# Summing the squares of three RMS norms with one strided VectorE reduction in place of seven GpSimd additions each

## The chip, the cores and the metric

The kernel runs on one core of one Trainium2 chip. The metric is the time of one execution on the device in microseconds (us); lower is better. The core has five engines that run side by side and wait for one another on semaphores: TensorE (PE in the profile, its weight loads are PEld), VectorE (DVE), ScalarE (ACT), GpSimd (POOL) and SyncE (SP), which issues most of the DMAs.

## The reference, cut to what matters

Three transformer blocks run one after the other on 512 tokens of width 1024, all in fp32: a differential attention block with an MLP, a latent attention block with an MLP, and a block of mixers with a gated MLP (SwiGLU) and a gated side input. Between them stand RMS norms over the 1024 features of a token:

```python
def rms_norm(x, g, eps=EPS):
    xf = x.astype(jnp.float32)
    y = xf * lax.rsqrt(jnp.mean(xf * xf, axis=-1, keepdims=True) + eps)
    return (y * g.astype(jnp.float32)).astype(x.dtype)

hn = rms_norm(h, attn_norm_g[0]); qkv = hn @ w_qkv_a[0]               # norm 0, first product
f = swiglu(rmsnorm(x, g_ffn_pre), w_gate_up, w_down)                  # norm 9, gate/up
gate = jax.nn.sigmoid(rmsnorm(x, g_ple) @ w_ple_gate)                 # norm 11, last gate
x = x + gate * (p @ w_ple_proj)
```

The change concerns how the sum of the squares of x over its features is made for these three norms (of twelve).

## The kernel before, in words

**Layout.** Activations lie transposed: the feature is the partition, and a tensor of 1024 features by 512 tokens is `h[128, 8, 512]`, eight tiles `h[:, k, :]` (KD = 8). An RMS norm is not applied ahead of its product. The product is made of the unscaled x, and the factor rstd, one number for each token, is multiplied into its result. So rstd is made while TensorE works, in these steps: eight tiles of squares (ACT); their sum over k, `ssq[128, 512]`; `stat` (L549): matmuls with a column of ones, which add up over the 128 partitions; `mean_square` (L1408, DVE); `rstd` (L2032, POOL, a power of -0.5); `broadcast` (L558): matmuls that spread rstd over all partitions; `take_rstd` (L1412, DVE), a copy into `rstd_f`.

**fp32 by three products.** Every operand is split into a high part of type fp32r and a low remainder. ACT makes the high part (`hi` L949 for weights, `x_hi` L961 for activations), DVE the low one (`lo` L1396, a `tensor_tensor` over 128x2048 at L1399; `x_lo` L1402, a `scalar_tensor_tensor` over 128x512 at L1405, eight for one norm). A product is three matmuls (L480 to L482). The first chunk of a stage goes in another order, as its x is fresh: for each k the two products with the high part of x (L519, L520), two output tiles at a time, and only then sixteen products with the low parts (L530), each pair behind its own `x_lo`.

**Weights.** They come in 149 chunks of 128x2048 fp32, each good for 48 matmuls, into two slots in turn. SP loads (L386), ACT writes `whi`, DVE writes `wlo`, TensorE waits for `wlo_done`. Each engine works through an order written out by hand; an engine that waits holds up all that is behind on it.

**Around the change.** In norms 0, 9 and 11 the order on TensorE is: first chunk c with its L530 tail; chunk c + 1, with `late_rstd` (L568) as a hook in it: `stat` ahead of its k = 3 (so behind 18 matmuls), and `broadcast` ahead of k = 4 for norm 0 and of k = 6 for norms 9 and 11. On DVE it is: eight `x_lo`; `lo(c + 1)`; for norm 0 some small operations (L1433 to L1442, one of them behind an exponential on ACT), `mean_square`, `lo(c + 2)`, `take_rstd`, two tables and a `rope`; for norms 9 and 11 `lo(c + 2)`, `mean_square`, `take_rstd` and the scaling of the product's tiles. On ACT the squares are L968 (norm 0) and L1329 (norms 9 and 11). On POOL `add_squares` (L2036) adds the tiles of squares one after another, seven additions at L2042, and ends with `rstd`; for norms 9 and 11 it stands behind four residual additions (L2171). The other norms are summed on POOL as well (norm 8 and 10 by `add_squares` too).

```python
for k in range(1, KD):
    pool.wait_ge(sq_done, SQ[n] + k + 1)
    if k >= 2:
        pool.wait_ge(ssq_done, SSQ[n] + k - 1)
    pool.tensor_tensor(ssq[:, :], squares[:, 0, :] if k == 1 else ssq[:, :], squares[:, k, :],
                       ALU.add).then_inc(ssq_done, 1)
rstd(n)
```

Of the kernel before, what the change touches and what calls it, by code (L numbers as in the profile page):

```python
# [16 lines left out]
ALU = mybir.AluOpType  # L17
ACT = mybir.ActivationFunctionType
AX = mybir.AxisListType
# [5 lines left out]
KD = D // P  # L25
# [47 lines left out]


SQUARED = (8, 8, 8, 2, 3, 8, 16, 0, 8, 8, 8, 8)
ADDED = (7, 7, 7, 1, 2, 7, 14, 0, 7, 7, 7, 7)
N_NORMS = len(SQUARED)
SQ = [sum(SQUARED[:n]) for n in range(N_NORMS + 1)]
SSQ = [sum(ADDED[:n]) for n in range(N_NORMS + 1)]
STATS = [n if n < 7 else n - 1 for n in range(N_NORMS)]  # L80
# [41 lines left out]
def build(nc, wst, xT, gains, cos, sin, ident_in, mask_in, lam, pT_in, tab_in, buckets_in, pool_w_in, pool_fix_in, outT):  # L122
    ctx = ExitStack()
    with ctx:
        def sem(name):
            return ctx.enter_context(nc.semaphore(name))
# [4 lines left out]
        def at(name, shape, dt, offset):  # L131
            return nc.alloc_sbuf_tensor_at(name, shape, dt, offset=offset)

        def sb(name, shape, dt=F32):
            n = (2 if dt == BF16 else 4) * int(np.prod(shape[1:]))
            t = at(name, shape, dt, base[0])
            base[0] += (n + 31) // 32 * 32
            assert base[0] <= top, (name, base[0], top)
            return t
# [14 lines left out]
        sq_tmp, ssq = sb("sq_tmp", [P, S]), sb("ssq", [P, S])  # L154
# [41 lines left out]
        squares0 = at("squares0", [P, KD, S], F32, xb_at + 16 * K)  # L196
# [15 lines left out]
        squares = at("squares", [P, KD, S], F32, G + 48 * K)  # L212
# [11 lines left out]
        squares2 = at("squares2", [P, KD, S], F32, G)  # L224
# [64 lines left out]
        sq_done = sem("sq_done")  # L289
        ssq_done = sem("ssq_done")  # L290
# [71 lines left out]
        def g(name, k):  # L362
            c0 = GAINS[name][0] + k
            return gain[:, c0:c0 + 1]
# [112 lines left out]
        def _(pe):  # L477
# [357 lines left out]
            def scores2(jb, tiles):  # L835

                q, k, _, hd = JOBS[jb]
                rows = slice(64 * (hd % 2), 64 * (hd % 2) + 64)
                for i in tiles:
                    tt = T_JOB[jb] + i  # L840
                    bank_ready(tt)
                    if jb % 2 == 0 and i == 0:
                        for tile in Q_TILES[jb // 2]:
                            pe.wait_ge(bank_free[tile % 4], tile // 4 + 1)
                    out, chosen = ps[tt % 4][:, 0:P * (i + 1)], jb >= 4 and i >= 1
                    mm = pe.matmul(out, q[rows, hd // 2, P * i:P * i + P], k[rows, hd // 2, 0:P * (i + 1)],  # L846
                                   start=True, stop=not chosen)
                    if chosen:
                        pe.wait_ge(sel_done, i)
                        mm = pe.matmul(out, ident_b[:, :], sel[:, IDX_OFF[i]:IDX_OFF[i] + P * (i + 1)],  # L850
                                       start=False, stop=True)
                    mm.then_inc(tile_done, 1)

            def weighted2(jb):
                _, _, v, hd = JOBS[jb]
                n = 2 * HEADS + jb
                if jb in (0, 4):
                    for tile in V_TILES[jb // 4]:
                        pe.wait_ge(bank_free[tile % 4], tile // 4 + 1)
                pe.wait_ge(on_done, HEADS + jb)  # L860
                for j, i in enumerate(TR_ORDER):
                    pe.wait_ge(ptc_done, 4 * n + j + 1)
                    for kt in range(i + 1):
                        mm = pe.matmul(O_PS[:, i * 64:(i + 1) * 64],  # L864
                                       pT2[:, OFF[i] + kt * P:OFF[i] + (kt + 1) * P],
                                       v[:, kt, 64 * hd:64 * hd + 64], start=(kt == 0), stop=(kt == i))
                mm.then_inc(o_done, 1)
# [527 lines left out]
        def _(dve):  # L1395
            def lo(c, slot):  # L1396

                dve.wait_ge(whi_done, c + 1)
                dve.tensor_tensor(wlo[slot][:, :], raw[slot][:, :], whi[slot][:, :].bitcast(F32),  # L1399
                                  ALU.subtract).then_inc(wlo_done, 1)  # L1400

            def x_lo(dst, src, scale, dst_hi, n):  # L1402

                dve.wait_ge(xh_done, n + 1)
                dve.scalar_tensor_tensor(out=dst, in0=src, scalar=scale, in1=dst_hi.bitcast(F32),  # L1405
                                         op0=ALU.mult, op1=ALU.subtract).then_inc(xl_done, 1)

            def mean_square(n, dim):  # L1408
                dve.wait_ge(stat_done, STATS[n] + 1)
                dve.tensor_scalar(ms_t[:, 4 * n:4 * n + 4], STAT[:, 0:QT], 1.0 / dim, EPS, ALU.mult, ALU.add).then_inc(ms_done, 1)  # L1410

            def take_rstd(n, dst=None):  # L1412
                dve.wait_ge(bc_done, n + 1)
                dve.tensor_copy((rstd_f if dst is None else dst)[:, :], BC[:, :]).then_inc(rstd_f_done, 1)
                dve.wait_ge(rstd_f_done, n + 1 - (n > 8) - (n > 10))

            def tile_ready(t, per=0, i=0):
                dve.wait_ge(tile_done, t + 1 + per * i)
# [8 lines left out]
            for k in range(KD):  # L1427
                x_lo(xa_lo[:, k, :], h[:, k, :], g("attn0", k), xa_hi[:, k, :], X["qkv"] + k)
            lo(1, 1)
            dve.wait_ge(const_loaded, 16 * len(consts))  # L1430

            for j in range(2):
# [23 lines left out]
            c, t = C["qk"], T["qk"]  # L1456
# [29 lines left out]
            c = C["v"]  # L1486
# [134 lines left out]
            c, t = C["dkv"], T["dkv"]  # L1621
# [40 lines left out]
            c, t = C["ukv"], T["ukv"]  # L1662
# [8 lines left out]
            c, t = C["uq"], T["uq"]  # L1671
# [55 lines left out]
            c, t = C["w_in"], T["w_in"]  # L1727
# [139 lines left out]
            c = C["att2"]  # L1867
# [44 lines left out]
            c, t = C["w_out"], T["w_out"]  # L1912
# [29 lines left out]
            def gate_up(r, n, first):  # L1942
                c, t = C[f"gu{r}"], T[f"gu{r}"]

                def pair(i):
                    for s in range(2):
                        j = HID2 + 8 * r + 2 * i + s
                        if not (first and isinstance(i, int) and s == 1):
                            lo(c + s + 1 + 2 * i, (c + s + 1) % 2)
                        if first and isinstance(i, int) and s == 0:  # L1950
                            lo(c + 2, c % 2)
                            mean_square(9, D)
                            take_rstd(9)
                        tt = t + 2 * s
                        tile_ready(tt, 4, i)
                        if not (first and isinstance(i, int)):
                            dve.wait_ge(hid_sq, j - 1)
                        dve.tensor_tensor(gate_t[:, s, :], ps[tt % 4][:, :], rstd_f[:, :], ALU.mult)\
                            .then_inc(bank_free[tt % 4], 1)
                        tile_ready(tt + 1, 4, i)  # L1960
                        dve.tensor_tensor(up_t[:, s, :], ps[(tt + 1) % 4][:, :], rstd_f[:, :], ALU.mult)\
                            .then_inc(bank_free[(tt + 1) % 4], 1)

                pair(0)
                with dve.Fori(1, n // 2) as i:
                    pair(i)
# [22 lines left out]
            c, t = C["ple"], T["ple"]  # L1989
# [2 lines left out]
                dve.wait_ge(gated_done, k + 1)  # L1992
                dve.tensor_tensor(h[:, k, :], h[:, k, :], projected[:, k, :], ALU.add).then_inc(y_done, 1)

            for j in (1, 2):
                lo(c + j, (c + j) % 2)
            mean_square(11, D)
            take_rstd(11)
            for u in range(4):
                for a in range(2):  # L2000
                    k, tt = 2 * u + a, t + 2 * u + a
# [18 lines left out]
        def _(pool):  # L2020
# [11 lines left out]
            def rstd(n):  # L2032
                pool.wait_ge(ms_done, n + 1)
                pool.tensor_tensor(rstd_t[:, 4 * n:4 * n + 4], ms_t[:, 4 * n:4 * n + 4], half_neg[:, :], ALU.pow).then_inc(rstd_t_done, 1)

            def add_squares(squares, n):  # L2036
# [7 lines that stand above are left out]
                rstd(n)  # L2044

            pool.wait_ge(dve_const, 1)
            add_squares(squares0, 0)


            def rope(t, dst1, dst2, rope_tmp, per=0, i=0):  # L2050
# [117 lines left out]
            def onto_residual(n0, n):  # L2168
                for k in RES_POOL:
                    pool.wait_ge(branch_done, KD * n0 + k + 1)  # L2170
                    pool.tensor_tensor(h[:, k, :], h[:, k, :], branch[:, k, :], ALU.add).then_inc(res_pool, 1)  # L2171
                add_squares(squares2, n)

            add_squares(squares2, 8)
            onto_residual(0, 9)
# [176 lines left out]
```

## Time and profile before

| what | value |
|---|---|
| median of 3 runs | 1928.97 us |
| lowest and highest run | 1926.86 and 1934.68 us |
| span of the profiled execution, first to last instruction | 1933.0 us |
| TensorE busy | 1890.8 us, 98% of the span |
| VectorE busy | 913.0 us, 47% |
| ScalarE busy | 615.6 us, 32% |
| GpSimd busy | 573.1 us, 30% |
| mean granted TensorE clock | 0.978 of full speed |

The profiled execution is an execution of its own. Its span is 4.0 us above the median and 1.7 us below the highest run; what it took outside of the span is not shown apart. Busy shares are means over the whole span: TensorE is the engine that sets the time nearly everywhere, and a wait of a few microseconds at one place does not show in its 98%. So the stretches around the three norms have to be read one by one.

### The profile page before, as it was taken

To read this page: it belongs to the slowest core of one execution; us is meant where nothing else is said; L and a number is where in the kernel's file an instruction comes from. 1 tells how busy PE (TensorE), PEld (TensorE's weight loads), DVE (VectorE), ACT (ScalarE), POOL (GpSimd) and SP (SyncE) were. 2 spreads that over 40 slices of the span, in tenths; PEclk is the share of its full clock that TensorE was granted. 3 is DMA by queue.
4 is the path that set the end of the run, shared out by engine and by line. 5 is a ranking of instruction groups with operands and counts; after the bars stand their busy time and mean duration, and the time that the engine had idled before them with its cause. 6 is when DMAs were issued, how large, how long until landed. Compare 5 with 4: busy or idle time off the path is not lost.

```text
span 1933.0 us, 22792 instructions
## 1 busy us (share of the span) xinstructions
PE 1890.8 (98%) x8694; PEld 1521.2 (79%) x8694; DVE 913.0 (47%) x1124; ACT 615.6 (32%) x886; POOL 573.1 (30%) x365
## 2 busy tenths in 40 slices
PE   8999999999999999999999999999998999999988
PEld 6796778888888886688888888777776788888866
DVE  6644654333333765453333334498555332333365
ACT  3235643121222434423122223233344222222342
POOL 3310246240515531054142235332024220211252
PEclk8997899999999999999999999999999899999998
DMA  4433412322223233234332322311121232222221
GB/s 170 142 109 80 106 66 87 107 90 96 100 87 104 85 111 111 78 109 105 102 109 87 108 87 87 136 66 66 44 77 66 87 107 89 95 101 88 108 87 66
DMA packets 40558, 183.94 MB, mean 95 GB/s; under 512 B 5512, under 2 KB 12200, under 8 KB 21416
## 3 DMA queue, kind: packets, MB, share of 16 engines
q1 hardware_dynamic: 38224, 179.26, 27.3%
q10 hardware_dynamic: 2264, 3.72, 1.0%
q8 instruction: 47, 0.77, 0.2%
q14 instruction: 23, 0.19, 0.0%
HBM read 161.99 MB, written 3.67 MB: 86 GB/s over the span
## 4 chain that ended last, share of the span: by engine, by line
PE 89%; DVE 6%; POOL 2%; ACT 1%; issue 1%; DMA 1%; SPq 0%; DVEq 0%; ACTq 0%; POOLq 0%
PE ps L480 22%; PE ps L482 22%; PE ps L481 22%; PE ps L530 3%; PE ps L520 3%; PE ps L519 3%; PE ps L656 2%; PE ps L643 1%; DVE xb L1405 1%; PE ps L760 1%; PE ps L667 1%; PE ps L846 1%; PE ps L864 1%; PE ps L770 1%; PE ps L642 1%
## 5 line engine op out<-in xcount | busy, mean ns | idle before, releaser
L1399 DVE TENSOR_TENSOR wlo<-raw,whi 128x2048 fp32r<-128x2048 f32 x142 | 351.1, 2472 | 324.7 <-ACT whi L955 324.4
L955 ACT ACTIVATE whi<-raw 128x2048 fp32r<-128x2048 f32 x149 | 284.4, 1909 | 384.5 <-PE ps L482 274.5
L480 PE MATMUL ps<-xb,whi 128*128 128x512 f32 x1024 | 402.9, 393 | 2.8 <-DVE wlo L1399 1.6
L481 PE MATMUL ps<-xb,whi 128*128 128x512 f32 x1024 | 400.3, 391 | 0.0
L482 PE MATMUL ps<-xb,wlo 128*128 128x512 f32 x1024 | 400.2, 391 | 0.0
L480 PE MATMUL ps<-xa_hi,whi 128*128 128x512 f32 x788 | 309.2, 392 | 3.9 <-DVE wlo L1399 3.8
L482 PE MATMUL ps<-xa_hi,wlo 128*128 128x512 f32 x788 | 308.3, 391 | 0.0
L481 PE MATMUL ps<-xa_lo,whi 128*128 128x512 f32 x788 | 308.3, 391 | 0.0
L480 PEld LDWEIGHTS ps<-xb,whi 128*128 128x128 f32 x1024 | 193.5, 189 | 45.8 <-issue 3.3
L482 PEld LDWEIGHTS ps<-xb,wlo 128*128 128x128 f32 x1024 | 193.3, 189 | 40.7
L481 PEld LDWEIGHTS ps<-xb,whi 128*128 128x128 f32 x1024 | 193.4, 189 | 40.0 <-issue 0.2
L2095 POOL TENSOR_TENSOR u_sq<-u_tmp 128x512 f32<-128x512 f32 x64 | 66.5, 1040 | 386.0 <-DVE u_tmp L1601 386.0
L480 PEld LDWEIGHTS ps<-xa_hi,whi 128*128 128x128 f32 x788 | 149.0, 189 | 36.0 <-DVE wlo L1399 5.1
L482 PEld LDWEIGHTS ps<-xa_hi,wlo 128*128 128x128 f32 x788 | 148.9, 189 | 31.2
L481 PEld LDWEIGHTS ps<-xa_lo,whi 128*128 128x128 f32 x788 | 149.0, 189 | 30.9
L1582 DVE TENSOR_TENSOR h<-ps,h 128x512 f32<-128x512 f32 x80 | 54.0, 690 | 189.5 <-PE ps L482 144.1
L1601 DVE SCALAR_TENSOR_TENSOR u_tmp<-ps,rstd_f 128x512 f32<-128x512 f32 x64 | 43.6, 691 | 143.0 <-PE ps L482 141.2
L2188 POOL TENSOR_TENSOR hid_t<-silu_t,up_t 128x512 f32<-128x512 f32 x22 | 28.3, 1285 | 236.9 <-ACT silu_t L1355 120.6
L519 PE MATMUL ps<-xa_hi,whi 128*128 128x512 f32 x188 | 73.5, 391 | 1.1 <-ACT xa_hi L962 1.1
L520 PE MATMUL ps<-xa_hi,wlo 128*128 128x512 f32 x188 | 73.2, 389 | 0.0
L2098 POOL TENSOR_TENSOR xb<-u_sq,xb 128x512 fp32r<-128x512 f32 x32 | 70.4, 2199 | 2.5
L2098 POOL TENSOR_TENSOR xa_lo<-u_sq,xa_hi 128x512 fp32r<-128x512 f32 x32 | 68.4, 2137 | 2.5
(309 smaller groups left out, 2555.1 us busy)
## 6 DMA issues: line engine op xcount, KB each, us to landing
raw<-wst SPq DMA_DIRECT2D x149, 1024.0 KB, 4.8
stage<-qk_split SPq DMA_DIRECT2D x64, 128.0 KB, 2.4
h<-xT ACTq DMA_DIRECT2D x4, 512.0 KB, 8.0
stage_k_lo<-qk_split SPq DMA_DIRECT2D x32, 64.0 KB, 2.0
mla_qn<-q_nope SPq DMA_DIRECT2D x8, 256.0 KB, 2.7
mla_v<-v_tok SPq DMA_DIRECT2D x8, 256.0 KB, 2.7
outT<-h SPq DMA_DIRECT2D x8, 256.0 KB, 2.0
bias_scratch<-bias_rows ACTq DMA_DIRECT2D x1, 1536.0 KB
```

Source lines behind the costliest of these rows:

```text
L480: pe.matmul(out, lhs_hi, rhs_hi, start=first, stop=False)
L481: pe.matmul(out, lhs_hi, rhs_lo, start=False, stop=False)
L482: return pe.matmul(out, lhs_lo, rhs_hi, start=False, stop=last)
L519: pe.matmul(out, w_hi[:, k, m], xhi[:, k, :], start=(k == 0), stop=False)
L520: pe.matmul(out, w_lo[:, k, m], xhi[:, k, :], start=False, stop=False)
L530: mm = pe.matmul(ps[(t0 + a) % 4][:, :], w_hi[:, k, m], xlo[:, k, :], start=False, stop=(k == kt - 1))
L955: act.activation(whi[slot][:, :], raw[slot][:, :], ACT.Copy).then_inc(whi_done, 1)
L1399: dve.tensor_tensor(wlo[slot][:, :], raw[slot][:, :], whi[slot][:, :].bitcast(F32), ALU.subtract).then_inc(wlo_done, 1)
L1582: dve.tensor_tensor(h[:, k, :], ps[t % 4][:, :], h[:, k, :], ALU.add).then_inc(bank_free[t % 4], 1)
L1601: dve.scalar_tensor_tensor(out=u_tmp[:, a, :], in0=ps[tt % 4][:, :], scalar=0.0, in1=rstd_f[:, :], op0=ALU.max, op1=ALU.mult)\
L2095: pool.tensor_tensor(u_sq[:, a, :], u_tmp[:, a, :], u_tmp[:, a, :], ALU.mult).then_inc(hid_sq, 1)
L2098: pool.tensor_tensor(hlo[:, j, :], u_sq[:, a, :], hhi[:, j, :].bitcast(F32), ALU.subtract)\
```

## The change

Three calls of `add_squares` on POOL go, and a new function `sum_squares` on DVE sums the eight tiles in one `tensor_reduce`. It reads the squares through a view in which k is the innermost axis: for each of 512 tokens eight numbers that lie 512 elements (2048 bytes) apart. It waits until all eight tiles are there. POOL keeps `rstd`. The semaphore's counts go from seven to one for these norms. On DVE the new call stands behind `lo(c + 1)` and, in norms 9 and 11, ahead of `lo(c + 2)`; in norm 0 it is ahead of the small operations.

```diff
-ADDED = (7, 7, 7, 1, 2, 7, 14, 0, 7, 7, 7, 7)
+ADDED = (1, 7, 7, 1, 2, 7, 14, 0, 7, 1, 7, 1)
@@ DVE
+            def sum_squares(squares, n):
+
+                dve.wait_ge(sq_done, SQ[n] + KD)
+                dve.tensor_reduce(ssq[:, :], squares[:, :, :].rearrange("p k n -> p n k"), AX.X, ALU.add).then_inc(ssq_done, 1)
+
@@ DVE, norm 0
             lo(1, 1)
+            sum_squares(squares0, 0)
             dve.wait_ge(const_loaded, 16 * len(consts))
@@ DVE, norm 9, in gate_up
                         if first and isinstance(i, int) and s == 0:
+                            sum_squares(squares2, 9)
                             lo(c + 2, c % 2)
                             mean_square(9, D)
@@ DVE, norm 11
-            for j in (1, 2):
-                lo(c + j, (c + j) % 2)
+            lo(c + 1, (c + 1) % 2)
+            sum_squares(squares2, 11)
+            lo(c + 2, c % 2)
             mean_square(11, D)
@@ POOL, norm 0
-            add_squares(squares0, 0)
+            rstd(0)
@@ POOL, norms 9 and 11, in onto_residual
-                add_squares(squares2, n)
+                rstd(n)
```

## Rows read from the trace of the kernel before

**Rows 1.** Page, part 4: the chain that ended last, by engine.
```profile
PE 89%; DVE 6%; POOL 2%; ACT 1%; issue 1%; DMA 1%; SPq 0%; DVEq 0%; ACTq 0%; POOLq 0%
```

**Rows 2.** Chain in order of time, 0 to 50 us: start, length, what.
```profile
26.87 5.54 issue
```

**Rows 3.** Timeline, DVE, norm 0: start, length, operation, [idle before, releaser].
```profile
11.49 9.54 DVE L1405 SCALAR_TENSOR_TENSOR xa_lo<-h,gain,xa_hi 128x512 fp32r<-128x512 f32 x8
...
14.14 3.50 DVE L1405 SCALAR_TENSOR_TENSOR xa_lo<-h,gain,xa_hi 128x512 fp32r<-128x512 f32 x2
...
20.95 3.36 DVE L1399 TENSOR_TENSOR wlo<-raw,whi 128x2048 fp32r<-128x2048 f32 x1
24.24 1.29 DVE L1433 CUSTOM_DVE_ANT_0 lam_in<-lam_in 128x64 f32<-128x64 f32 x1
```

**Rows 4.** Timeline, ACT, norm 0.
```profile
17.79 2.18 ACT L968 ACTIVATE squares<-h 128x512 f32<-128x512 f32 x4
...
43.84 1.92 ACT L955 ACTIVATE whi<-raw 128x2048 fp32r<-128x2048 f32 x1 [16.12 <-PE ps L482]
```

**Rows 5.** POOL: L2042's minimum, median and maximum in ns; timeline of norm 0, then 9.
```profile
L2042 POOL TENSOR_TENSOR ssq<-ssq,squares x30: 1274/1383/3139, 15.6 to 1883.9; 128x512 f32<-128x512 f32 x30
...
15.64 11.23 POOL L2042 TENSOR_TENSOR ssq<-ssq,squares 128x512 f32<-128x512 f32 x6 [0.26 <-ACT squares L968]
32.45 3.00 POOL L2034 TENSOR_TENSOR rstd_t<-ms_t,half_neg 128x4 f32<-128x4 f32 x1 [5.58 <-DVE ms_t L1410]
...
1491.29 8.04 POOL L2042 TENSOR_TENSOR ssq<-ssq,squares 128x512 f32<-128x512 f32 x5 [0.37 <-ACT squares L1329]
1510.63 1.02 POOL L2034 TENSOR_TENSOR rstd_t<-ms_t,half_neg 128x4 f32<-128x4 f32 x1 [11.30 <-DVE ms_t L1410]
```

**Rows 6.** Timeline, PE, norm 0.
```profile
24.37 0.80 PE L480 MATMUL ps<-xa_hi,whi 128*128 128x512 f32 x1 [2.55 <-DVE wlo L1399]
...
31.22 0.95 PE L555 MATMUL ps<-ones,ssq 128*128 128x1 f32 x8
...
35.60 1.13 PE L564 MATMUL ps<-ident,rstd_t 128*128 128x128 f32 x8 [1.95 <-POOL rstd_t L2034]
```

**Rows 7.** Timeline, DVE, norm 9.
```profile
1487.99 12.56 DVE L1405 SCALAR_TENSOR_TENSOR xb<-h,gain,xb 128x512 fp32r<-128x512 f32 x8
1500.46 2.28 DVE L1399 TENSOR_TENSOR wlo<-raw,whi 128x2048 fp32r<-128x2048 f32 x1
```

**Rows 8.** Timeline, PE, norm 9.
```profile
1490.28 0.61 PE L530 MATMUL ps<-xb,whi 128*128 128x512 f32 x2
...
1502.80 0.80 PE L480 MATMUL ps<-xb,whi 128*128 128x512 f32 x1 [0.79 <-DVE wlo L1399]
...
1509.40 0.95 PE L555 MATMUL ps<-ones,ssq 128*128 128x1 f32 x8
...
1514.44 1.05 PE L564 MATMUL ps<-ident,rstd_t 128*128 128x128 f32 x8
```

**Rows 9.** Timeline, norm 11: DVE, then PE.
```profile
1874.13 12.55 DVE L1405 SCALAR_TENSOR_TENSOR xb<-h,gain,xb 128x512 fp32r<-128x512 f32 x8
...
1888.94 0.80 PE L480 MATMUL ps<-xb,whi 128*128 128x512 f32 x1 [0.79 <-DVE wlo L1399]
...
1900.40 1.05 PE L564 MATMUL ps<-ident,rstd_t 128*128 128x128 f32 x8
```

**Rows 10.** DVE groups by form: tensor_reduce at two widths; busy us, mean ns.
```profile
L1502 DVE TENSOR_REDUCE negmin<-ps 128x1 f32<-128x512 f32 x16 | 11.0, 690 | 7.8 <-PE ps L630 7.8
...
L1502 DVE TENSOR_REDUCE negmin<-ps 128x1 f32<-128x128 f32 x16 | 4.7, 291 | 21.7 <-PE ps L630 21.5
```

**Rows 11.** Timeline, PE, norms 8 and 10: broadcasts behind a wait.
```profile
1476.79 1.67 PE L564 MATMUL ps<-ident,rstd_t 128*128 128x128 f32 x8 [1.91 <-POOL rstd_t L2034]
...
1863.45 1.16 PE L564 MATMUL ps<-ident,rstd_t 128*128 128x128 f32 x8 [1.82 <-POOL rstd_t L2034]
```

**Rows 12.** Busy time by engine in a window, then granted clock, DMA share, GB/s.
```profile
1477.00:1480.90 3.90, 3.90 (x14) 2.91 (x13) 2.37 (x4) 0.60 (x1) 0.19 (x1) 0.56 0.82 267
```

## The prediction

> **What bounds the kernel now.** I read the page's chain first: TensorE carries 89% of it [rows 1], so only what lets TensorE start sooner or run at a better clock counts. Then I read the chain around norm 0, and it misleads: it runs through POOL's additions, then has 5.54 us of "issue" [rows 2] ahead of POOL's next operation. That operation was late because `stat` was; `stat` stood behind 18 matmuls and found `ssq` long ready: POOL's additions ended at 26.87 (15.64 + 11.23) [rows 5], `stat` ran at 31.22 [rows 6]. So the third view, each engine's timeline, decides. TensorE waits 2.55 us for `wlo` of chunk c + 1 [rows 6], and DVE is late with it since its eight `x_lo` and the `lo` behind them are slow. The first four `x_lo` start 0.66 us apart (11.49 to 14.14: 2.65 for four); from 14.14, when POOL has begun to add, two take 3.50 [rows 3]. In norms 9 and 11 all eight run beside POOL's additions and take 12.56 and 12.55 [rows 7, 9], 1.57 each; POOL's five take 8.04, 1.6 each [rows 5]. The two engines go in lockstep, one blocking the other. `lo` shows it too: 3.36 us beside POOL [rows 3], 2.28 without [rows 7].
>
> **The change, part by part.** It takes POOL out of that stretch and puts one long reduction on DVE behind `lo(c + 1)`, where it is no longer in front of what TensorE waits for first.
>
> *Price of the reduction.* A reduction over 512 elements takes 690 ns, over 128 291 ns [rows 10]: 1.04 ns an element and 0.16 fixed, so 4096 elements take 4.43 us. These rows read neighbouring elements. No row reads at a stride of 2048 bytes; that could cost more. The far bound is the seven additions that it replaces, the nearest rows in which tiles this far apart are summed: at the quickest 1274 ns each [rows 5], 8.9 us, counted as 9.0. I take 4.43, nearest by operation and engine, and keep 9.0. The lower bound is the same 4.43; a quicker one gains at most the 0.3 us of wait named below.
>
> The Trainium skill ("SBUF — State Buffer", The DMA port swizzle, note on cachelines) says that SBUF is read in lines of 16 bytes and that an access pattern which goes to a new line with every element pays a penalty. Here every element is in a new line. No row can show it; by it the reduction would be near the far bound and the total that of the second rival below.
>
> *Norm 9.* `x_lo` starts at 1487.99 as before, all of its inputs ready. Eight at 0.66 end at 1493.35; `lo(c + 1)` at 2.28 ends at 1495.6. TensorE has its 16 L530 matmuls done by 1493.9 (from 1490.28, at 0.23 each) and starts chunk c + 1 at 1495.65 instead of 1502.80 [rows 8]: **7.15 us**. Then 18 matmuls to `stat`. Before they took 6.60 (1502.80 to 1509.40), though at the full clock 18 take 4.1 (1514.44 less 1509.40 less 0.95 for `stat` itself) [rows 8]. The low clock came from the crumbs of work between the waits for `x_lo`. Now the reduction ends 4.45 behind the chunk's start, so `stat` waits 0.35 us; `broadcast` is at 4.5 + 0.95 + 4.1 = 9.55 behind the start instead of 11.64 (1514.44 - 1502.80): **2.1 us** more. rstd must be there: the reduction, then `lo(c + 2)` 2.28, now ahead of `mean_square`, then 0.2, then POOL's 1.02 [rows 5]: 8.1 behind the start, in time. What is queued behind the reduction on DVE is `lo(c + 2)`, wanted only 11 us after the chunk's start. Sum 9.25.
>
> *Norm 11* is the same code shape: `x_lo` from 1874.13, start of chunk c + 1 at 1881.8 instead of 1888.94 (7.1), broadcast at 9.55 behind it instead of 11.46 (1900.40 - 1888.94): 1.9 [rows 9]. Sum 9.0.
>
> *Norm 0.* `x_lo` ends at 16.9 (11.49 + 8 x 0.66; its last input is ready by 16.0, as ACT then has the 1.9 us of `whi` [rows 4] still to do ahead of the squares at 17.79). `whi` is complete by 17.9, so `lo(1)` ends at 20.2; TensorE's L530 tail ends there too, and chunk c + 1 starts at 20.3 instead of 24.37 [rows 6]: 4.1. The squares are complete at 19.97 [rows 4], the reduction ends at 24.65, `stat` at 25.6. Behind the reduction on DVE are the small operations, which end at about 26.0 if the 1.29 us of the first [rows 3] was POOL's doing, 27.1 if not; `mean_square` follows, then POOL's power. That took 3.00 us beside `lo(c + 2)` and 1.02 without [rows 5]; `whi(c + 2)` stands on ACT behind the exponential, which waits for the first small operations (25.1 at the soonest), and takes 1.9, so `lo(c + 2)` can't start before 27.3 and the power takes 1.02. `broadcast` at 27.3 instead of 35.60 [rows 6]: 8.3. The rest of chunk c + 1 took 7.3 us before (35.60 + 0.9 to 43.84, when ACT sees its tiles done [rows 4]) for 24 matmuls that take 5.5 at the full clock: 1.8. Against it: `rope` frees the banks for the next chunk 0.3 late, as `take_rstd` now stands behind `lo(c + 2)`. Sum 9.8.
>
> *Costed at nothing:* the removed POOL additions themselves (nothing waits for POOL here); the DMAs, of which the same are issued (the weights' loads only wait for `wlo_done`, which comes sooner); ACT's order, unchanged.
>
> Total 9.8 + 9.25 + 9.0 = 28.1 us. It is worked out in the profiled execution, whose span of 1933.0 becomes 1904.9; against the median of 1928.97 that gives **1900.9, said as 1901 us**. This is 1.5%; 0.5%, 9.6 us, is about what a measurement can tell from none.
>
> **Rivals.**
>
> *The clock stays low in norms 9 and 11 (0.11).* TensorE still idles 1.7 us ahead of chunk c + 1. Idle of 1.91 us was followed by a granted clock of 0.56, idle of 1.82 was not followed by slow matmuls [rows 11, 12]. If it falls, the second terms (2.1 and 1.9) go: 24.1 us gained, 1905.
>
> *The strided read costs double (0.12).* The reduction takes 9.0. Norm 9: start still 7.15 sooner, `stat` 9.0 behind it, TensorE idle for 4.9 and at the low clock after (2.5 more, the 6.60 against 4.1): broadcast 16.5 behind the start instead of 11.64, net 2.3; norm 11 net 2.0; norm 0 broadcast at 32.0, net 3.6. Sum 7.9: 1921. Against it: 4.43 is what the engine takes when fed. For it: nothing here reads so.
>
> *Slower (0.06).* The one mechanism is the same reduction at four times 4.43, 17.7 us, on DVE in front of `stat`. Norm 9: broadcast at 17.7 + 0.95 + 4.1 + 2.5 = 25.3 behind the start instead of 11.64, less 7.15: 6.5 lost; norm 11 6.7; norm 0 5.8. Sum 19: 1948. It decides from 11.2 us on (7.15 + 11.64 - 7.55), 2.5 times the contiguous rate, more than even the far bound.
>
> *The change doesn't free DVE (0.03).* If `x_lo` is slow for another reason than POOL, nothing moves: 4.43 is less than the 6.60 until `stat`. 1929. Rows 3 speak against: the pace changes just as POOL starts.
>
> **How the numbers follow.** The forecast as worked out has 0.68. Of the double price's 0.12, 0.05 lies below 1.9 times, where over 9.6 us are still gained. Faster: 0.68 + 0.11 + 0.05 = 0.84; same: 0.07 + 0.03 = 0.10; slower: 0.06. The range is 1896 (5 us for the spread of runs and for `lo` and `x_lo` quicker than counted) to 1915, which takes in 1905 and reductions up to 1.6 times the price, in all 0.82.
>
> **What would show it.** In the profile after: `x_lo` at 0.66 apart in the three norms; `lo(c + 1)` 2.28; a TENSOR_REDUCE of `ssq` x3 at 4.4 us; `stat` waiting for it by under 0.5; POOL's rstd of norm 0 at 1.0 instead of 3.0; clock near 1.0 in chunk c + 1. Wrong if the reduction is over 6 us, if `x_lo` keeps 1.5, or if TensorE's idle time turns up at `stat` or `broadcast`.

## The result and the profile after

The changed kernel takes 1918.19 us (median of four runs, 1913.09 to 1920.82) against 1931.83 of the kernel before in the same comparison (1926.86 to 1934.77): a ratio of 0.9929, 95% interval 0.9903 to 0.9954, so 13.6 us or 0.7% faster. The prediction was 1901 with a range of 1896 to 1915: the sign is right, the size is half of what was forecast, and the median lies 3.2 us outside the range. 2.9 of these 3.2 us are the base: the forecast was counted from a median of 1928.97, and this comparison's is 1931.83. The size of the gain doesn't depend on that. The profiled execution has a span of 1918.7 against 1933.0, 14.3 us less, and the places below are read in these two.

DVE's timeline in the changed kernel (start, length, operation, [idle before, releaser]), norm 0 and then norm 9:

```profile
11.29 5.38 DVE L1405 SCALAR_TENSOR_TENSOR xa_lo<-h,gain,xa_hi 128x512 fp32r<-128x512 f32 x8
17.72 2.29 DVE L1399 TENSOR_TENSOR wlo<-raw,whi 128x2048 fp32r<-128x2048 f32 x1 [1.04 <-ACT whi L955]
19.93 7.30 DVE L1411 TENSOR_REDUCE ssq<-squares 128x512 f32<-128x4096 f32 x1
...
1482.84 5.38 DVE L1405 SCALAR_TENSOR_TENSOR xb<-h,gain,xb 128x512 fp32r<-128x512 f32 x8
1488.14 2.28 DVE L1399 TENSOR_TENSOR wlo<-raw,whi 128x2048 fp32r<-128x2048 f32 x1
1490.35 7.30 DVE L1411 TENSOR_REDUCE ssq<-squares 128x512 f32<-128x4096 f32 x1
1497.58 2.27 DVE L1399 TENSOR_TENSOR wlo<-raw,whi 128x2048 fp32r<-128x2048 f32 x1
```

The eight `x_lo` take 5.38 us where they took 9.54 and 12.56 [rows 3, 7], and `lo(c + 1)` is at its 2.28. The new operation takes 7.30 us, not 4.43. TensorE's timeline shows both, in the same two places and at the end in norm 11:

```profile
20.07 0.50 PE L480 MATMUL ps<-xa_hi,whi 128*128 128x512 f32 x1
...
27.29 1.42 PE L555 MATMUL ps<-ones,ssq 128*128 128x1 f32 x8 [2.80 <-DVE ssq L1411]
...
31.27 1.91 PE L564 MATMUL ps<-ident,rstd_t 128*128 128x128 f32 x8
...
1490.48 0.50 PE L480 MATMUL ps<-xb,whi 128*128 128x512 f32 x1 [1.47 <-DVE wlo L1399]
...
1497.70 1.05 PE L555 MATMUL ps<-ones,ssq 128*128 128x1 f32 x8 [2.85 <-DVE ssq L1411]
...
1504.39 1.05 PE L564 MATMUL ps<-ident,rstd_t 128*128 128x128 f32 x8
...
1508.02 0.39 PE L480 MATMUL ps<-xb,whi 128*128 128x512 f32 x1
...
1872.19 0.50 PE L480 MATMUL ps<-xb,whi 128*128 128x512 f32 x1 [1.48 <-DVE wlo L1399]
...
1886.15 1.05 PE L564 MATMUL ps<-ident,rstd_t 128*128 128x128 f32 x8
```

Chunk c + 1 starts at 20.07 instead of 24.37 [rows 6]. In norm 9 the time from the first `x_lo` to the chunk's start is 7.64 us instead of 14.81 [rows 7, 8], 7.17 less. Then `stat` waits 2.8 to 2.9 us for the reduction in each of the three norms, and afterwards TensorE is slow. The next two lines are windows of the changed kernel in norm 9: chunk c + 1 up to `stat`, and from `stat` to `broadcast`. Behind the window's length stand the busy times of PE, PEld, DVE, ACT and POOL, each with its number of instructions, then the granted clock, the DMA share and GB/s:

```profile
1490.50:1497.70 7.20, 4.35 (x18) 3.28 (x19) 7.20 (x2) 1.80 (x2) 0.00 (x0) 1.00 0.42 146
1497.70:1504.40 6.70, 6.70 (x27) 5.56 (x28) 2.22 (x2) 0.00 (x0) 1.02 (x1) 0.75 0.46 157
```

18 matmuls are done in the first 7.2 us at a clock of 1.00, the engine then stands still for 2.85 us, and behind that the clock falls: part of the second window runs at the lower level of 1.2 GHz, mean 0.75. In norm 0 the mean is 0.54 from 27.3 to 34.0 us. Who waited for whom on TensorE, over the whole of the changed kernel:

```profile
PE ps L555 <- DVE ssq L1411: 8.5, 3, 2.9
PE ps L564 <- POOL rstd_t L2042: 4.0, 3, 1.9
PE ps L480 <- DVE wlo L1399: 3.8, 3, 1.5
```

Each line gives us in total, times, longest. The first line is the new wait: 8.5 us in three. What the change gave at each place, from the two profiled executions:

| place | forecast | found | how found |
|---|---|---|---|
| norm 0, end of chunk 1 | 9.8 | 4.4 | ACT sees its tiles at 39.42 (line below) instead of 43.84 [rows 4] |
| norm 9, first `x_lo` to `broadcast` | 9.25 | 4.9 | 21.55 us instead of 26.45 [rows 7, 8] |
| norm 11, first `x_lo` to `broadcast` | 9.0 | 4.7 | 1864.56 to 1886.15 is 21.59 instead of 26.27 [rows 9] |

```profile
39.42 1.92 ACT L955 ACTIVATE whi<-raw 128x2048 fp32r<-128x2048 f32 x1 [9.87 <-PE ps L482]
```

The three make 14.0 of the 14.3 us of the spans, which is closer than single executions allow. Of norm 0's 4.4, 0.2 is only an earlier start of the whole execution (first `x_lo` at 11.29 instead of 11.49). And the same code between the places takes more or less from one execution to the next. Behind the broadcast of norm 8 the next stage starts 5.52 us later in the kernel before (clock 0.69) and 3.94 in the changed one (clock 1.00); behind that of norm 10 it is 3.94 and 5.51. Here these two differences cancel.

### The profile page after: what moved, and what is told of

Same layout as the page of the kernel before. It is cut to its first block, busy times and chain, and to the rows that moved or that the text cites. A ratio compares the mean times of both kernels' runs of the same rounds, so it can differ in the third digit from the quotient of the medians.

```text
span 1918.7 us, 22752 instructions
## 1 busy us (share of the span) xinstructions
PE 1878.9 (98%) x8690; PEld 1517.7 (79%) x8694; DVE 913.5 (48%) x1127; ACT 615.8 (32%) x886; POOL 538.5 (28%) x344
## 4 chain that ended last, share of the span: by engine, by line
PE 90%; DVE 6%; ACT 1%; POOL 1%; DMA 1%; issue 1%; SPq 0%; DVEq 0%; ACTq 0%; POOLq 0%
PE ps L480 23%; PE ps L481 22%; PE ps L482 22%; PE ps L530 3%; PE ps L519 3%; PE ps L520 3%; PE ps L656 2%; PE ps L643 1%; PE ps L760 1%; DVE ssq L1411 1%; PE ps L846 1%; PE ps L667 1%; PE ps L864 1%; PE ps L770 1%; PE ps L642 1%; DVE wlo L1399 1%
```

## Experiments

**The reduction by itself.** Ten forms of the same operation, run one after another behind the end of the changed kernel, where the core has nothing else to do. One execution.

```diff
+            for j, (out, src) in enumerate((
+                    (ssq[:, :], h[:, :, :].rearrange("p k n -> p n k")),
...
+                    (ssq[:, 0:2], flat.rearrange("p (k b) -> p b k", b=2)))):
+                if j:
+                    dve.wait_ge(form_done, j)
+                dve.tensor_reduce(out, src, AX.X, ALU.add).then_inc(form_done, 1)
```

> The changed kernel with ten more reductions of h on VectorE behind its last addition, each alone and behind a semaphore: strided groups of 8 (512 outputs, 2048 bytes between elements), of 4 and of 2 tiles; contiguous groups of 8 (512 outputs), of 64 and one of 4096; then 4096 elements at a stride of 256, 64, 16 and 8 bytes in long groups (64, 16, 4 and 2 outputs). Theory S, the reads cost: all contiguous forms take 4.4 us, whatever the number of outputs, the first takes 7.3, and long groups at a stride of 16 bytes or more are slow as well. Theory G, the groups cost: each of the 512 outputs costs (7.30 - 4.43)/512 = 5.6 ns on top of 1.04 ns an element, so contiguous groups of 8 take 7.3 us, groups of 64 4.8, one group 4.4, and the strided long groups 4.4 to 4.8; strided groups of 4 tiles take 2.3 + 2.9 = 5.2, of 2 tiles 4.1 (by theory S 3.7 and 1.9).

DVE's timeline of that run; the order is the one in the expectation:

```profile
1916.29 7.03 DVE L2042 TENSOR_REDUCE ssq<-h 128x512 f32<-128x4096 f32 x1
1923.36 3.62 DVE L2042 TENSOR_REDUCE ssq<-h 128x512 f32<-128x2048 f32 x1
1927.01 1.23 DVE L2042 TENSOR_REDUCE ssq<-h 128x512 f32<-128x1024 f32 x1
1928.28 4.42 DVE L2042 TENSOR_REDUCE ssq<-h 128x512 f32<-128x4096 f32 x1
1932.73 4.42 DVE L2042 TENSOR_REDUCE ssq<-h 128x64 f32<-128x4096 f32 x1
1937.19 4.42 DVE L2042 TENSOR_REDUCE ssq<-h 128x1 f32<-128x4096 f32 x1
1941.64 6.99 DVE L2042 TENSOR_REDUCE ssq<-h 128x64 f32<-128x4096 f32 x1
1948.66 6.98 DVE L2042 TENSOR_REDUCE ssq<-h 128x16 f32<-128x4096 f32 x1
1955.68 7.32 DVE L2042 TENSOR_REDUCE ssq<-h 128x4 f32<-128x4096 f32 x1
1963.03 4.42 DVE L2042 TENSOR_REDUCE ssq<-h 128x2 f32<-128x4096 f32 x1
```

Contiguous groups take 4.42 us whether there are 512 outputs, 64 or one (4th to 6th line). So theory G falls, and the forecast's price was right to 0.01 us for contiguous reads. Strides of 16, 64 and 256 bytes take 7.0 to 7.3 in long groups, 8 bytes 4.42 (7th to 10th): the reads cost, theory S. It had one thing wrong: with two tiles the stride of 2048 bytes costs nothing (1.23 for 1024 elements; theory S had 1.9), with four it does (3.62 for 2048).

**The same reads made contiguous in place.**

```diff
-                dve.tensor_reduce(ssq[:, :], squares[:, :, :].rearrange("p k n -> p n k"), AX.X, ALU.add).then_inc(ssq_done, 1)
+                near = squares[:, :, :].rearrange("p k n -> p (k n)").rearrange("p (n k) -> p n k", k=KD)
+                dve.tensor_reduce(ssq[:, :], near, AX.X, ALU.add).then_inc(ssq_done, 1)
```

> The three reductions read groups of 8 neighbouring elements in place of 8 elements 2048 bytes apart, so that the sums are of other elements than the norm's; the work is otherwise that of the changed kernel. Theory S (the stride costs): the reduction takes 4.4 us, stat waits under 0.5 us for it in norms 9 and 11, the gain on the kernel before is the 24 to 28 us of the prediction. Theory G (the 512 groups cost): 7.3 us, and the time is that of the changed kernel, 13 to 14 us under the kernel before.

The sums are of other elements than the norm's, so the output is not that of the reference; the run is for its times. Ratio 0.9850 on the kernel before, 95% interval 0.9833 to 0.9866; medians 1901.94 and 1931.19, 29 us, slightly over the 24 to 28 expected. DVE, then TensorE, in norm 9 of this run, and last ACT behind norm 0's chunk:

```profile
1481.73 4.41 DVE L1412 TENSOR_REDUCE ssq<-squares 128x512 f32<-128x4096 f32 x1
...
1481.87 0.50 PE L480 MATMUL ps<-xb,whi 128*128 128x512 f32 x1 [1.48 <-DVE wlo L1399]
...
1486.19 1.05 PE L555 MATMUL ps<-ones,ssq 128*128 128x1 f32 x8
...
1491.32 1.05 PE L564 MATMUL ps<-ident,rstd_t 128*128 128x128 f32 x8
...
33.62 1.92 ACT L955 ACTIVATE whi<-raw 128x2048 fp32r<-128x2048 f32 x1 [6.96 <-PE ps L482]
```

The reduction takes 4.41, `stat` comes 4.3 us behind the chunk's start with no wait to speak of, and `broadcast` 9.45 behind it (the forecast had 9.55). By places, measured as in the table above, it gains 10.2, 9.4 (1474.23 to 1491.32 instead of 26.45 us) and 9.2 (1851.03 to 1868.13 instead of 26.27), where the forecast had 9.8, 9.25 and 9.0. One access pattern decides 2.9 us of one operation and, through it, half of the gain.

**Three contiguous additions on VectorE**, the version that a user can have: the sums are the norm's. The first two additions write over the squares.

```diff
-ADDED = (1, 7, 7, 1, 2, 7, 14, 0, 7, 1, 7, 1)
+ADDED = (3, 7, 7, 1, 2, 7, 14, 0, 7, 3, 7, 3)
...
-                dve.tensor_reduce(ssq[:, :], squares[:, :, :].rearrange("p k n -> p n k"), AX.X, ALU.add).then_inc(ssq_done, 1)
+                for j, m in enumerate((4, 2)):
+                    if j:
+                        dve.wait_ge(ssq_done, SSQ[n] + j)
+                    dve.tensor_tensor(squares[:, 0:m, :], squares[:, 0:m, :], squares[:, m:2 * m, :],
+                                      ALU.add).then_inc(ssq_done, 1)
+                dve.wait_ge(ssq_done, SSQ[n] + 2)
+                dve.tensor_tensor(ssq[:, :], squares[:, 0, :], squares[:, 1, :], ALU.add).then_inc(ssq_done, 1)
```

> The reduction becomes three tensor_tensor additions on VectorE over whole contiguous halves (4 tiles onto 4, 2 onto 2, 1 onto 1: 2048, 1024 and 512 elements). By the durations of the same operation at these widths they take 2.28 + 1.23 + 0.69 = 4.2 us. If the price of the reduction and the clock that falls behind its wait are all that the forecast had wrong, this gives 24 to 28 us on the kernel before. If the fall in the clock comes from the 1.5 us idle ahead of chunk c + 1 or something else, it gives only the 3 us of each reduction, 13.6 + 9 = 22 us at most.

Ratio 0.9845 (0.9828 to 0.9863), medians 1901.88 and 1931.19: 29 us. That is slightly over the 24 to 28 expected, and clearly over the 22 that it would have been at most if the clock had fallen for another reason. DVE's timeline in norm 9 and the windows up to `stat` and from it to `broadcast`:

```profile
1481.81 3.54 DVE L1414 TENSOR_TENSOR squares<-squares 128x2048 f32<-128x2048 f32 x2
1485.38 0.69 DVE L1417 TENSOR_TENSOR ssq<-squares 128x512 f32<-128x512 f32 x1
```

```profile
1481.90:1486.20 4.30, 4.26 (x19) 3.38 (x19) 4.23 (x4) 1.85 (x2) 0.00 (x0) 1.00 0.66 238
1486.20:1491.20 5.00, 5.00 (x27) 4.31 (x27) 2.15 (x2) 0.00 (x0) 1.02 (x1) 1.00 0.39 110
```

They take 4.26 us in all (1481.81 to 1486.07), and the clock stays at its upper level, although TensorE has the same 1.5 us idle ahead of the chunk as in the changed kernel. So that idle does not bring it down; what is gone here is the wait at `stat`. This kernel is faster than both the kernel before and the changed one, and as fast as e2.

**GpSimd's additions, later.**

```diff
             def add_squares(squares, n):
+
+                if n in (0, 9, 11):
+                    pool.wait_ge(wlo_done, C[{0: "qk", 9: "gu0", 11: "ple"}[n]] + 2)
```

> The kernel before, seven additions on GpSimd as they were, but they wait until lo(c + 1) is done. Theory L (GpSimd's additions hold up x_lo while both run): x_lo starts 0.66 us apart in the three norms and chunk c + 1 starts 7.15 us sooner in norms 9 and 11 and 4 us in norm 0, though VectorE has no reduction; the additions then come late, stat some 9 to 11.5 us behind the chunk's start, broadcast 16 to 18 behind it in place of 11.6, and the whole is 2 to 6 us under the kernel before. Rival theory (the gain has to do with VectorE's own order or with ssq, not with GpSimd beside it): x_lo stays at 1.57 us and the time is over that of before by the late additions.

All seven additions of each of the three norms now wait until `lo(c + 1)` is done. DVE, POOL and TensorE in norm 9 of this run:

```profile
1487.38 5.38 DVE L1405 SCALAR_TENSOR_TENSOR xb<-h,gain,xb 128x512 fp32r<-128x512 f32 x8
...
1496.47 10.17 POOL L2045 TENSOR_TENSOR ssq<-ssq,squares 128x512 f32<-128x512 f32 x6
...
1506.70 1.87 PE L555 MATMUL ps<-ones,ssq 128*128 128x1 f32 x8 [7.31 <-POOL ssq L2045]
```

With POOL out of the way and no reduction on DVE, `x_lo` again takes 5.38 in all three norms, and in norms 9 and 11 chunk c + 1 starts 7.63 us behind the first of them: POOL's additions beside them were the cause of the slow stretch. But the additions now end late, `stat` waits 7.31 us, and the ratio is 1.0001 (0.9992 to 1.0011): everything won at the chunk's start is paid back at `stat`. The 2 to 6 us expected did not come. `stat` is 11.7 us behind the chunk's start, just past what was expected, and `broadcast` is 20.3 us behind it in norm 9 and 19.5 in norm 11 (1882.62 to 1902.08) instead of 16 to 18. From `stat` to `broadcast` it takes 8.6 and 7.7 us at a clock of 0.57 and 0.65, where e2 has 5.1; the low clock behind so long a wait was not in that sum. It takes both, POOL away and a sum quick enough to be there for `stat`.

**`stat` later, reduction as changed.**

```diff
-                if k == 3:
+                if k == (3 if norm == 0 else 6):
                     stat(norm)
-                elif k == (4 if norm == 0 else 6):
+                elif k == (4 if norm == 0 else 7):
```

> The changed kernel with its strided reduction of 7.3 us, but in norms 9 and 11 stat stands ahead of k = 6 instead of k = 3 and broadcast ahead of k = 7 instead of k = 6. Theory W (what the long reduction costs is TensorE's wait of 2.85 us at stat and the low clock behind it): stat comes 8.3 us behind the chunk's start without a wait, rstd is there at 10.9, broadcast at 11.0 behind the start instead of 13.9, the clock stays at its upper level, and the time is 5 to 6 us under the changed kernel, 19 to 20 under the kernel before. Rival theory (the reduction costs by something else, such as what it holds up on VectorE): the time stays within 2 us of the changed kernel's.

Ratio 0.9893 (0.9866 to 0.9921), medians 1911.18 and 1928.36. TensorE in norm 9, and a window over the stretch:

```profile
1490.37 0.50 PE L480 MATMUL ps<-xb,whi 128*128 128x512 f32 x1 [1.47 <-DVE wlo L1399]
...
1498.69 0.95 PE L555 MATMUL ps<-ones,ssq 128*128 128x1 f32 x8
...
1501.16 1.16 PE L564 MATMUL ps<-ident,rstd_t 128*128 128x128 f32 x8
...
1504.51 0.47 PE L480 MATMUL ps<-xb,whi 128*128 128x512 f32 x1 [0.79 <-DVE up_t L1968]
```

```profile
1488.00:1500.00 12.00, 10.53 (x50) 8.42 (x49) 12.00 (x5) 3.24 (x3) 0.00 (x0) 1.00 0.25 87
```

`stat` does not wait, the clock is 1.00, `broadcast` stands 10.8 us behind the chunk's start instead of 13.9. From the first `x_lo` to the start of chunk c + 2 norm 9 takes 21.78 us (1482.73 to 1504.51) instead of 25.18 (1482.84 to 1508.02), norm 11 21.79 instead of 25.25: 6.9 us for both, though the reduction takes 7.50 us here. Theory W holds. The medians, from two comparisons, say the same more roughly: 17 us under the kernel before by the medians and 21 by the ratio, against 13.6 for the changed kernel. A part is handed on: rstd is late enough for the next chunk to wait 0.79 us for a bank, and in norm 9 e2 is still 1 us shorter (20.71).

**Norm 0 alone.** The edit is the change's own lines for norm 0, with `ADDED` 1 at that place only.

> The kernel before with the change at norm 0 alone. If the three places add up, as the traces say, it gives 4.4 us, a ratio of 0.9977; chunk 1 starts near 20.1 instead of 24.4, broadcast is near 31.3 instead of 35.6. If most of the 13.6 us came from a common cause, it differs from that by more than 2 us.

Ratio 0.9971 (0.9953 to 0.9989), medians 1923.15 and 1928.36, 5.2 us; chunk 1 starts at 20.16, `broadcast` is at 30.97. This agrees with the 4.4 us expected, but the interval goes from 2 to 9 us, so it can't settle a difference of 2. The trace shows how far a single execution can be trusted. Norm 0's place gives 5.9 us here (ACT at 37.90) and 4.4 in the changed kernel, with the same code: the clock behind `stat` was 0.75 and 0.54 from 27.3 to 34.0 us. And this execution reaches norm 9's `x_lo` 11.8 us before the kernel before does (1476.19 and 1487.99), 5.9 more than norm 0 explains.

**The power ahead of `lo` in norms 8 and 10**, on top of the three additions.

```diff
                 mean_square(n, D)
+                dve.wait_ge(rstd_t_done, n + 1)
                 lo(c_next, c_next % 2)
```

> The kernel with three contiguous additions on VectorE (e3), and in norms 8 and 10 lo(c_next) waits until GpSimd's power is done. The power takes 1.0 us instead of 3.0, TensorE's idle of 1.9 us ahead of broadcast goes, VectorE's lo ends 1.1 us later and its scaling of branch starts 0.8 us sooner. Gain on e3: 1.6 us for both norms by VectorE's start, up to 4 if the clock fell behind these waits; 0 if lo becomes what the scaling waits for by more than counted.

Ratio 0.9835 (0.9804 to 0.9867), which can't be told from e3's 0.9845. TensorE in norm 8:

```profile
1463.16 1.16 PE L564 MATMUL ps<-ident,rstd_t 128*128 128x128 f32 x8
...
1467.72 0.47 PE L519 MATMUL ps<-xb,whi 128*128 128x512 f32 x1 [1.99 <-ACT xb L962]
...
1469.64 0.79 PE L519 MATMUL ps<-xb,whi 128*128 128x512 f32 x1 [0.76 <-ACT xb L962]
```

The power takes 1.02 us instead of 3.00 and the wait at `broadcast` is gone, but the next one, for the first fresh tiles, has grown from 1.4 to 2.0 us, and the clock behind it is 0.61 (1467 to 1475) where e3 has 1.00. The trace still shows a gain. From norm 8's `stat` to the first `x_lo` of norm 9 it takes 14.15 us (1460.68 to 1474.83) instead of e3's 15.15, from norm 10's to norm 11's 14.08 instead of 15.08, and both are still ahead at the next `broadcast`. That is 2 us for both norms, near the 1.6 expected, and too little for the ratios to tell.

**Six more views of the reduction.**

```diff
+                    (ssq[:, :], h[:, 0:3, :].rearrange("p k n -> p n k")),
+                    (ssq[:, :], h[:, 0:8:7, :].rearrange("p k n -> p n k")),
+                    (ssq[:, :], h[:, 0:2, :].rearrange("p k n -> p n k")),
+                    (ssq[:, 0:3], flat[:, 0:4095].rearrange("p (k b) -> p b k", b=3)),
+                    (ssq[:, 0:256], h[:, :, :].rearrange("p k (m t) -> p m k t", t=2)),
+                    (ssq[:, 0:128], h[:, :, :].rearrange("p k (m t) -> p m k t", t=4)))):
```

> As e1, behind the end of the changed kernel, with six other views of h: groups of 3 tiles; of tiles 0 and 7; of tiles 0 and 1 again; a stride of 12 bytes in long groups; 256 groups of 16, where two neighbouring tokens are read from each of the eight tiles in turn; 128 groups of 32 with four neighbouring tokens. e1 had 1.04 ns an element for strides of 4 and 8 bytes and for groups of 2 tiles, and 1.67 to 1.75 for 16 bytes and more and for groups of 4 and 8 tiles. Theory A (a 16-byte line must be hit twice within a few accesses, whatever comes between): 3 tiles are slow (1.7 ns, 2.8 us), tiles 0 and 7 as fast as 0 and 1 (1.23 us), 12 bytes lies between or is slow (4.4 to 7.0 us), two or four neighbours from each tile are read at the full rate (4.4 us). Theory B (it is the distance of 2048 bytes, which for two tiles happens to be hidden): tiles 0 and 7 are slow (1.9 us), two neighbours from each tile still cost more than 5 us.

DVE's timeline, in the order of the edit:

```profile
1909.51 1.91 DVE L2038 TENSOR_REDUCE ssq<-h 128x512 f32<-128x1536 f32 x1
1911.46 1.23 DVE L2038 TENSOR_REDUCE ssq<-h 128x512 f32<-128x1024 f32 x1
1912.72 1.23 DVE L2038 TENSOR_REDUCE ssq<-h 128x512 f32<-128x1024 f32 x1
1913.99 5.53 DVE L2038 TENSOR_REDUCE ssq<-h 128x3 f32<-128x4095 f32 x1
1919.55 4.42 DVE L2038 TENSOR_REDUCE ssq<-h 128x256 f32<-128x4096 f32 x1
1924.01 4.42 DVE L2038 TENSOR_REDUCE ssq<-h 128x128 f32<-128x4096 f32 x1
```

Tiles 0 and 7 are as quick as 0 and 1, and two or four neighbouring tokens from each of eight tiles are read at the full rate: theory B falls. Theory A holds but for its figure for three tiles, which take 1.91 us, 1.14 ns an element (1.912 less 0.16 fixed, by 1536), where 2.8 was expected; a stride of 12 bytes takes 5.53, 1.31 ns an element.

## Why the prediction was wrong

*What bounds the kernel* was right in its main point. The chain's share of POOL's additions misled, and the timelines showed what held TensorE: `x_lo` and `lo` beside POOL. E4 shows it with no other part of the change present.

*The start of chunk c + 1* was right: 7.15 forecast, 7.17 found in norm 9; 7.1 and 7.2 in norm 11 (1864.56 to 1872.19 instead of 1874.13 to 1888.94: 7.18 less); 4.1 and 4.3 in norm 0.

*The price of the reduction* is the step that failed. The prediction had 4.43 us, "nearest by operation and engine", from rows that read neighbouring elements (of `ps`, which is in PSUM; e1 shows the same 4.42 for neighbouring elements of SBUF, so the memory was not the error). It is 7.30, 1.65 times that. The second part of the step is the clock behind the wait at `stat`, which the sum put at nothing. By the stretch of norm 9, the reduction's 2.9 us move `stat` by 2.9 us (7.2 behind the chunk's start instead of 4.3 in e2), and the clock adds 1.6: from the start of `stat` to `broadcast` 6.69 us against 5.13 in e2. Together 4.5 a norm, where forecast and result differ by 4.4 and 4.3. In norm 0 `broadcast` is at 31.27 instead of 27.3, and the low clock lasts into the rest of the chunk: 5.4. These are the 14 us. With the price put right nothing of size is missing: e2 and e3 gain 29 us in the median, the forecast was 28.1, and each place of e2 is within 0.5 us of its forecast.

*The rule of the Trainium skill* ("SBUF — State Buffer", The DMA port swizzle, note on cachelines) was the better guide. It says that each access that goes to a new line of 16 bytes pays. The trace agrees for the case at hand, 7.30 against 4.42. It does not hold in general: in e1 and e8 a read that changes to another tile, and so to another line, with every element goes at the full rate when there are two tiles (1.23 us for 1024 elements). The prediction gave the rival that the strided read costs double 0.12. It worked out 9.0 us as 7.9 us gained; with 7.30 in the same three sums, 1.7 us less in each, it would have been 13.0, which is close to the 13.6 and 14.3 measured. So the mechanism of this rival is what happened, at two thirds of its surcharge. The range ended at 1.6 times the price, and the measured one is 1.65.

*The other rivals.* The clock did fall in norms 9 and 11, but not for the reason given: 1.5 us idle ahead of the chunk left it at 1.00 in the changed kernel, in e2 and in e3; 2.85 us at `stat` did not. The length of a wait is not all that decides: the 1.91 us ahead of norm 8's broadcast are followed by a clock of 0.69 in the kernel before and of 1.00 in the changed one. "Slower" would have needed 11.2 us. "The change doesn't free DVE" is excluded by `x_lo` at 5.38.

*The smaller terms.* POOL's power in norm 0 takes 1.02 us, as forecast, instead of 3.00 [rows 5]; the first of the small operations takes 0.21 instead of 1.29 [rows 3], so its length had been POOL's doing. In e4, where POOL adds later, that first one takes 0.22 and two others, now beside the additions, take 0.89 and 1.32 instead of 0.16 and 0.22.

## What to carry to other kernels

Price an operation by a row with the same access pattern, not only the same engine and operation; where none is there and a rule speaks against the pattern, that rule deserves more than a small chance. To add up eight tiles on VectorE, halve them with wide contiguous additions (4.26 us here) rather than reduce through a transposed view (7.30), if the tiles may be overwritten. Moving work off an engine that another one contends with pays at the place where it was in the way, and is paid back at the next consumer if the moved work comes late: look for that consumer first.

## What the runs showed of the hardware that was not expected

A VectorE reduction reads fp32 from SBUF at 1.04 ns an element at strides of 4 and 8 bytes, at 1.31 at 12 bytes, and at 1.67 to 1.75 at 16, 64 and 256 bytes, all in long groups. It is not the jump to another line as such that costs: alternating between two distant tiles goes at the full rate, three cost 1.14, four 1.69 (3.62 us less 0.16, by 2048), eight 1.68 (7.03 us). Two neighbouring elements from each of eight tiles in turn are at the full rate again. Theory A of the last experiment fits these times but for three tiles; the runs show the times, not the mechanism. The same reduction takes 7.03 us on an otherwise idle core and 7.27 to 7.50 beside TensorE and ACT; this was not followed up.
